# First-stage loads, squares and copies reordered, and the meta keys' V products paired in 64-row halves, in a Hymba encoder block on 8 cores

## The reference

```python
h = rms_norm(x, norm_g)
u, g_pool, q, k, v, g_na = split(h @ w_in)                 # 1024 columns each
pool_out = pool_mixer(u, w_pool, pool_scale) * silu(g_pool)
# per query: softmax over 16 meta keys and a window of 8 rows x 16 columns of a grid 64 wide
p = softmax(concat([s_meta, s_grid]))                       # 16 heads of 64
na_out = (p_m @ vm + p_g @ v_window) * silu(g_na)
y = rms_norm(x + concat([pool_out, na_out]) @ w_out, final_g)
```

## Time and profile before

| what | value |
|---|---|
| median of 3 runs | 1763.38 us (1757.53 to 1893.18) |
| the profiled execution | 1761.12 us |
| its span, slowest core (core 0) | 1759.6 us |
| spans of the 8 cores | 1748.7 to 1759.6 us |
| mean granted TensorE clock of core 0 | 0.986 of full speed |
| busy: PE, DVE, ACT, POOL | 96%, 57%, 47%, 7% |
| attention stage, as the windows cut it | 442 to 1059 us |

### The profile page before, as it was taken

One profiled execution on the slowest core, in us unless ns is written; L12 is line 12 of the kernel. 1 busy time (PEld: TensorE's weight loads), 2 busy tenths in 40 slices (PEclk: granted clock), 3 DMA queues, 4 the chain that ended last, 5 costly groups with the idle time before them and its releaser, 6 DMA issues.

```text
span 1759.6 us, 39346 instructions; the slowest of 8 cores (1748.7 to 1759.6 us)
## 1 busy us (share of the span) xinstructions
PE 1690.0 (96%) x13906; PEld 873.7 (50%) x13906; DVE 1000.9 (57%) x1907; ACT 821.3 (47%) x1219; POOL 124.3 (7%) x202
## 2 busy tenths in 40 slices
PE   7799999999999899999999998999999999999998
PEld 3344544444455555655666554444444444444443
DVE  3354544442466665766777755556655566556654
ACT  3256666331256765777777762332333233323332
POOL 1011021111100000000000020000000000000000
PEclk9899999999999999999999999999999999999999
DMA  9689778663555566666543479733454346524521
GB/s 264 218 239 282 226 240 238 200 169 136 172 141 157 149 166 176 154 179 176 146 123 98 132 214 266 187 114 109 126 174 148 86 128 162 168 88 129 139 96 61
DMA packets 163814, 289.21 MB, mean 164 GB/s; under 512 B 70627, under 2 KB 92643, under 8 KB 155047
## 3 DMA queue, kind: packets, MB, share of 16 engines
q1 hardware_dynamic: 110167, 155.04, 31.2%
q0 software_dynamic: 37184, 95.66, 19.1%
q10 hardware_dynamic: 16272, 35.99, 6.6%
HBM read 194.90 MB, written 100.90 MB: 168 GB/s over the span
## 4 chain that ended last, share of the span: by engine, by line
PE 79%; issue 5%; ACT 5%; DVE 4%; DMA 4%; SPq 2%; ACTq 1%; DVEq 0%; POOL 0%; POOLq 0%
PE bankpair L433 19%; PE bankpair L927 9%; PE bankpair L588 9%; PE bankpair L620 9%; PE bankpair L407 9%; PE bankpair L380 9%; PE bankpair L904 5%; PE bankpair L1039 3%; PE bankpair L1008 3%; ACT sb_PT L1014 2%; DMA sb_XSG<-xt 2%; DVE sb_PT L1020 1%; PE bankpair L567 1%; PE bankpair L368 1%; DVE sb_QT L217 1%
## 5 line engine op out<-in xcount | busy, mean ns | idle before, releaser
L1014 ACT ACTIVATE sb_PT<-bankpair 128x1024 bf16<-128x1024 f32 (+1 forms) x368 | 318.8, 921 | 152.8 <-PE bankpair L1008 112.1
L433 PE MATMUL bankpair<-sb_Wo,sb_MIX 128*128 128x512 bf16 x1536 | 336.9, 381 | 3.7 <-DVE sb_MIX L417 3.7
L433 PEld LDWEIGHTS bankpair<-sb_Wo,sb_MIX 128*128 128x128 bf16 x1536 | 150.8, 98 | 187.8 <-issue 9.1
L1020 DVE TENSOR_TENSOR sb_PT<-sb_PT,sb_FT 128x1024 bf16<-128x1024 bf16 (+1 forms) x264 | 174.8, 666 | 106.1 <-ACT sb_PT L1014 103.3
L927 PE MATMUL bankpair<-sb_Wz,sb_HT 128*128 128x512 bf16 x768 | 199.6, 388 | 3.0 <-ACT sb_PM L957 2.7
L588 PE MATMUL bankpair<-sb_HT,sb_Wk 128*128 128x512 bf16 (+1 forms) x832 | 189.7, 383 | 9.5 <-ACT sb_Wk L219 5.0
L904 PE MATMUL bankpair<-sb_HT,sb_Wq 128*128 128x512 bf16 x768 | 194.7, 382 | 1.7 <-DVE sb_QT L217 1.7
L620 PE MATMUL bankpair<-sb_Wv,sb_HT 128*128 128x512 bf16 x816 | 184.0, 379 | 0.0
L380 PE MATMUL bankpair<-sb_HT,sb_Wg 128*128 128x512 bf16 x768 | 182.6, 381 | 0.0
L441 ACT ACTIVATE sb_junk<-sb_Y 128x1024 bf16<-128x1024 f32 x48 | 50.7, 1057 | 266.3 <-DVE sb_Y L436 266.3
L407 PE MATMUL bankpair<-sb_HT,sb_Wg 128*128 128x512 bf16 x768 | 167.7, 379 | 0.0
(11 more groups left out here) (104 smaller groups left out, 1736.3 us busy)
## 6 DMA issues: line engine op xcount, KB each, us to landing
sb_X<-xall SPq DMA_DIRECT2D x51, 512.0 KB, 5.7
sb_XR<-xall SPq DMA_DIRECT2D x48, 512.0 KB, 3.6
y<-sb_O POOLq DMA_DIRECT2D x48, 512.0 KB, 3.2
sb_HT<-hT_s SPq DMA_DIRECT2D x23, 1024.0 KB, 6.1
sb_KR<-kT_s SPq DMA_DIRECT2D x14, 1024.0 KB, 7.2
sb_UW<-u_s SPq DMA_DIRECT2D x54, 256.0 KB, 7.8
kT_s<-sb_KTs POOLq DMA_DIRECT2D x13, 1024.0 KB, 5.1
v_s<-sb_Vs POOLq DMA_DIRECT2D x49, 260.0 KB, 3.5
```

What stands on the lines that cost most here:

```text
L433: S.op('tensor', lambda e, po=po, kc=kc, cg=cg, j=j: e.matmul(banks[po][:, :], MIX[:, kc, j * 128:(j + 1) * 128], Wo[kc // 4][:, kc % 4, c ...
L1014: S.op('scalar', lambda e: e.activation(out=PT[ps][0:nk, bi, :, 0:n].rearrange('p (a b) q -> p a b q', a=2), in_=bank2[sp][0:nk, :].rearra ...
L1020: S.op('vector', lambda e: e.tensor_tensor(out=PT[ps][0:nk, bi, :, 0:n], in0=PT[ps][0:nk, bi, :, 0:n], in1=bl['E'](hs), op=ALU.mult), read ...
```

## The change

**Start of stage 1.** The constants' DMAs leave the start and go into the loop at its index 3 (the scaling of `psc` to index 7); `hT` of chunk 0 is written after the transposes of chunk 1 begin; the K products of chunk 0 and the transposes of chunk 1 are interleaved; the first V column group of chunk 0 is computed as soon as its two weights are there, then the first half of K of chunk 1, and then the second V column group. The fillers between chunk 1's transposes are gone. The SP queue has the same loads in the same order.

**Loop of stage 1.** `p1_front` is split: `p1_sum` (load, square, root) runs two row tiles ahead, `p1_scale` one ahead. `p1_HTevac` is issued directly behind the transposes, and no longer behind the K products and tables.

**Attention.** The heads' banks are now cut by halves (heads 0 to 3 and 4 to 7 of a G) in place of parity. The meta product of a unit becomes two matmuls of 64 rows and 260 columns, one in each half of the array, into banks 4 and 5, issued beside the K products. `pv_plan` takes the place of `pv_steps` and says, by the number of blocks of the next unit and by whether that unit begins a pair, where the meta products go, which product opens a bank, and in which step each half is done. The V products of the corner cells use 128 rows always, with the missing half of `VC` set to zero. The output's store goes on SP's queue for all tiles.

```diff
@@ -552,12 +550,19 @@
...
+
+        def p1_scale(ci, j):
+            xs, sc = tile_xs[(ci, j)], tile_sc[(ci, j)]
...
+
+        def p1_front(ci, j):
+            p1_sum(ci, j)
+            p1_scale(ci, j)
...
@@ -693,30 +698,42 @@
...
-        p1_consts()
+        p1_wcast(0)
+        p1_wcast(1)
+        p1_K(0, [0, 1])
+        p1_wcast(2)
+        p1_front(1, 0)
+        p1_K(0, [2, 3])
+        p1_wcast(3)
+        p1_front(1, 1)
+        p1_K(0, [4, 5])
+        p1_T(1, 0)
+        p1_K(0, [6])
+        p1_HTevac(1, 0)
+        p1_front(1, 2)
+        p1_T(1, 1)
+        p1_K(0, [7])
+        p1_HTevac(1, 1)
+        p1_front(1, 3)
+        p1_wcast(4)
+        p1_T(1, 2)
+        p1_HTevac(1, 2)
         p1_keep(0)
-        p1_wcast(0)
+        p1_sum(2, 0)
+        p1_wcast(5)
+        p1_VU(0, 0, (0,))
+        p1_T(1, 3)
+        p1_scale(2, 0)
+        p1_HTevac(1, 3)
+        for j in range(1, 4):
+            p1_VU(0, j, (0,))
+        p1_sum(2, 1)
+        p1_K(1, [0, 1])
+        p1_wcast(6)
+        p1_wcast(7)
+        p1_K(1, [2, 3])
         for j in range(4):
...
+            p1_VU(0, j, (1,))
...
@@ -725,22 +742,27 @@
             ntc = chunks[ci][1]
             nxt = order[idx + 1] if idx + 1 < len(order) else None
             ntn = chunks[nxt][1] if nxt is not None else 0
-            if idx > 1:
-                p1_keep(ci)
+            p1_keep(ci)
+            if idx == 3:
+                p1_consts()
+            if idx == 7:
+                S.op('vector', lambda e: e.tensor_scalar(out=psc[:], in0=psc[:], scalar1=0.5, scalar2=None, op0=ALU.mult),
+                     reads=['psc'], writes=['psc'])
             for j in range(4):
                 if j < ntn:
                     p1_T(nxt, j)
                     if (nxt, j) in after:
-                        p1_front(*after[(nxt, j)])
-                if idx > 1:
+                        p1_scale(*after[(nxt, j)])
+                        if after[(nxt, j)] in after:
+                            p1_sum(*after[after[(nxt, j)]])
+                    p1_HTevac(nxt, j)
+                if idx > 1 or j > 1:
                     p1_K(ci, [2 * j, 2 * j + 1])
                 if idx >= 2 and j % 2 == 1 and tpi < len(pieces):
                     p1_table(tpi); p1_table(tpi + 1)
                     tpi += 2
                     if tpi < len(pieces):
                         p1_tload(tpi); p1_tload(tpi + 1)
-                if j < ntn:
-                    p1_HTevac(nxt, j)
                 if j < ntc:
                     p1_VU(ci, j)
                 if idx in (4, 5):
@@ -1021,59 +1046,65 @@
                 out=PT[ps][0:nk, bi, :, 0:n], in0=PT[ps][0:nk, bi, :, 0:n], in1=bl['E'](hs), op=ALU.mult),
                  reads=[('PT', ps, bi), bl['eres']], writes=[('PT', ps, bi)])
-        def p2_pvmeta(ui, par):
+        def p2_pvmeta(ui, opens, ends=False):
             t, s, G = units[ui]
...
+            for half in range(2):
+                rows = slice(64 * half, 64 * half + 64)
+                S.op('tensor', lambda e, half=half, rows=rows: e.matmul(
+                    banks[4 + half][:, 0:260], PM[t % 2][rows, G, s, :], VMb[rows, G, 0:260],
+                    start=(opens or half == 1), stop=(ends and half == 0)), reads=[('PM', t % 2, G)] + VMR, writes=[PS(4 + half)])
+
+        def p2_pv(ui, half, bi, opens, last):
             t, s, G = units[ui]
-            n = TILES[t]['nq'] * 16
             ps = ui % 2
             bl = unit_blocks(units[ui])[bi]
-            nk = bl['nk']
-            for jj in range(4):
+            for q in range(4):
+                jj, par = 2 * half + q // 2, q % 2
                 h = 2 * (4 * G + jj) + par
...
+                S.op('tensor', lambda e, q=q, jj=jj, par=par, h=h: e.matmul(
+                    banks[4 + half][:, q * 65:(q + 1) * 65], PT[ps][:, bi, par * 4 + jj, :],
+                    bl['V'][:, h * 65:(h + 1) * 65], start=(opens and q == 0), stop=(last and q == 3)),
+                     reads=bl['vres'] + [('PT', ps, bi)], writes=[PS(4 + half)])
+
+        def p2_norm(ui, half):
             t, s, G = units[ui]
             tl = TILES[t]
             n = tl['nq'] * 16
             at = (ui // 2) % 2
-            ab = 4 + par
+            ab = 4 + half
             accv = lambda: banks[ab][0:n, 0:260].rearrange('p (a b) -> p a b', a=4)
-            rs = slice(par * 4, par * 4 + 4)
+            rs = slice(half * 4, half * 4 + 4)
+            c0 = (8 * G + 4 * half) * 64
             S.op('vector', lambda e: e.reciprocal(rec[0:n, rs], accv()[:, :, 64]),
-                 reads=[PS(ab)], writes=[('rec', par)])
+                 reads=[PS(ab)], writes=[('rec', half)])
             S.op('vector', lambda e: e.tensor_tensor(
-                out=ATT[at][0:n, :].rearrange('p (a b c) -> p a b c', a=8, b=2)[:, 4 * G:4 * G + 4, par, :], in0=accv()[:, :, 0:64],
+                out=ATT[at][0:n, c0:c0 + 256].rearrange('p (a c) -> p a c', a=4), in0=accv()[:, :, 0:64],
                 in1=rec[0:n, rs].unsqueeze(2).to_broadcast([n, 4, 64]), op=ALU.mult),
-                 reads=[PS(ab), ('rec', par)], writes=[('ATT', at)])
-            if G == 1 and par == 1:
+                 reads=[PS(ab), ('rec', half)], writes=[('ATT', at)])
+            if G == 1 and half == 1:
                 t0 = tl['t0']
-                late.append(lambda: S.op('gpsimd' if 9 <= t < 13 else 'sync', lambda e: e.dma_start(
+                late.append(lambda: S.op('sync', lambda e: e.dma_start(
                     out=at_d[t0:t0 + n * 4, :].rearrange('(r c) f -> r c f', c=64)[:, 16 * s:16 * s + 16, :], in_=ATT[at][0:n, :]),
                      reads=[('ATT', at)], writes=[('at_d', t, s)], dma=('sA', at)))
...
+        nblk = [len(unit_blocks(u)) for u in units]
+        first_step = [sum(nblk[:i]) for i in range(len(units))]
+
+        def pv_plan(ui):
+
+            nb = nblk[ui]
+            nn = nblk[ui + 1] if ui + 1 < len(units) else 2
+            even = ui + 1 == len(units) or first_step[ui + 1] % 2 == 0
+            opens = even and nn == 2
+            lead = [lambda bi=bi: p2_pv(ui, 0, bi, bi == 0 and not opens, False) for bi in range(nb - 1)]
+            tail = lambda last: [lambda: p2_pv(ui, 0, nb - 1, False, last)]
+            half1 = [lambda bi=bi: p2_pv(ui, 1, bi, False, bi == nb - 1) for bi in range(nb)]
+            n0, n1 = [lambda: p2_norm(ui, 0)], [lambda: p2_norm(ui, 1)]
+            if nn == 2:
+                return 0 if even else 1, opens, {0: lead, 1: tail(True) + n0 + half1 + n1}
+            if even:
+                return 2, False, {0: lead, 1: tail(False), 2: half1 + n1}
+            return 1, False, {0: lead, 1: tail(True) + n0 + half1[:2], 2: half1[2:] + n1}
         late = []
         for fc in range(KC):
@@ -1107,11 +1138,8 @@
             if b == 1:
                 while late:
                     late.pop(0)()
-            for f in pv_steps(ui - 1)[b] if ui > 0 and b < 3 else []:
+            for f in pv_plan(ui - 1)[2].get(b, []) if ui > 0 else []:
                 f()
...
             if b == nb - 1:
                 unit_end(ui)
@@ -1147,10 +1175,18 @@
             for ui, b in steps[k:k + 2]:
                 if b == 0:
                     unit_begin(ui)
+                if b == 2 and ui > 0 and pv_plan(ui - 1)[0] == 2:
+                    p2_pvmeta(ui - 1, False, True)
+                    p2_norm(ui - 1, 0)
+            for ui, b in steps[k:k + 2]:
                 p2_qk(ui, b)
             for ui, b in steps[k:k + 2]:
+                if b < 2 and ui > 0 and pv_plan(ui - 1)[0] == b:
+                    p2_pvmeta(ui - 1, pv_plan(ui - 1)[1])
+            for ui, b in steps[k:k + 2]:
                 unit_step(ui, b)
-        for part in pv_steps(len(units) - 1):
+        p2_pvmeta(len(units) - 1, True)
+        for part in pv_plan(len(units) - 1)[2].values():
             for f in part:
                 f()
         while late:
```

More of the change, by code:

```diff
@@ L241, in build_program @@
         second += [('VP0_%d' % q, [128, VW], BF16) for q in range(3)] + [('VC%d' % w, [128, VW], BF16) for w in range(2)]
-        second += [('VMb', [128, 2, 2, 4, 65], BF16), ('KM', [128, KC, 32], BF16), ('HTm', [128, KC, 128], BF16)]
+        second += [('VMb', [128, 2, 264], BF16), ('KM', [128, KC, 32], BF16), ('HTm', [128, KC, 128], BF16)]
         second += [('PM%d' % i, [128, 2, 4, 128], BF16) for i in range(2)]
@@ L491, in p1_consts @@
                     S.op('gpsimd', lambda e: e.dma_start(out=psc[:], in_=psT_d), writes=['psc'], dma='c6')
-                    S.op('vector', lambda e: e.tensor_scalar(out=psc[:], in0=psc[:], scalar1=0.5, scalar2=None, op0=ALU.mult),
-                         reads=['psc'], writes=['psc'])
                     S.op('gpsimd', lambda e: e.dma_start(out=mbP[:], in_=mbP_d), writes=['mbP'], dma='c9')
@@ L541, in p1_load, with p1_sum @@
                          writes=[('X', xs)], dma=('X', xs))
[L543 removed]
+                def p1_sum(ci, j):
                     if (ci, j) not in tile_xs:
```

(11 more changed lines are left out.)

44 lines of the change are left out of this document (removed).

## The result

The changed kernel is slower: its time is 1.0325 times that of before, with a 95% interval of 1.0304 to 1.0347. Its profiled execution took 1821.2 us, 60.1 more than the profiled execution of before (1761.1); the forecast was 1803. Two of its four executions were disturbed and are left out of the ratio.

A forecast was written before the change was run, and what follows sets the result against it. The prediction took the PE, busy 96% of the span, as the bound; -3 - 9 - 12.3 - 1.5 (corner products and mode switches) + 12 + 41 + 15 = +42 on 1761.1 gave 1803 us, own range 1790 to 1818, 8-in-10 range 1765 to 1832.

The forecast's parts named there:

- one wait as the decisive one: Attention, two-chunk tiles: V products of the moved second half wait for DVE's multiply of the next unit's block 0; +41 us.
- Rival 2: Attention: the block-0 wait doesn't bind, so the kernel is not slower; 1747 us, chance 0.08.
- rival 3: Whole kernel: every wait costs the clock (+34 us) and DMA gives nothing back at the start; 1831 us, chance 0.15.
- rival 1: Start, loop and clock: x comes in time and the clock mostly holds; 1782 us, chance 0.27.
- Rival 4: Attention: the two meta halves don't run together, +12 us on the forecast; 1815 us, chance 0.05.
- Banks opened early: Attention, tiles 0 and 4, 15 places: meta pairs right behind K products wait 1.0 us for the division; +12 us.
- Start: Start of stage 1: loads land earlier without the constants, but the PE idles 8 us awaiting chunk 2's x; -3 us.
- The constants at index 3: Loop of stage 1: constants loaded there have a whole chunk, 29 us, before the first fold needs Wp; no cost.
- Waits of the transposes: Loop of stage 1: the four waits for the HT copy go, with their clock loss; -9 us, bounds -4 and -11.
- Meta pairs: Attention: two 64-row halves run at once, so 112 products of 0.11 us are saved; -12.3 us.
- Clock: Attention: half of the 20 long block-0 waits drop the PE's clock; +15 us, bounds 0 and +34.
- "Other edits": Attention: zeroing half of VC and the store on SP's queue cost nothing, at worst 4 and 2 us.

The follow-up runs named there:

- slot3: The changed kernel, with block 0 of a pair's second step written to the free fourth buffer slot at s = 0 (12 of 24 places); 1798.6 us, ratio 1.0226.
- early_pair: The changed kernel, with the meta pair opening both banks in the first step also before 3-block units, blocks 0 and 1 read in step 1; 1811.0 us.
- stage1_only: The kernel before with the stage 1 edits alone, attention as before; 1760 us, ratio 0.9997.
- s1_early: stage1_only with the constants' DMAs at index 2, ahead of the WuT loads, and the HT copy ahead of the scaling on DVE; 1752.6 us, ratio 0.9933.
- best1: s1_early with ACT's table pieces behind p1_VU and the memsets of KM, PM and VMb on POOL; 1747.4 us, ratio 0.9900.
- mid_full: Stage 1 of before, changed attention, but at 39 places two 128-row meta products, each before its half, blocks 0 and 1 read in step 1; ratio 1.0065.
- full_all: mid_full with no meta product paired: all 112 units use two products of 128 rows; ratio 1.0039.
- best_pair: best1 with the attention of mid_full and VC[0] of tile 0 zeroed on POOL; 1749.8 us, ratio 0.9922.

## Why the prediction was right, and which terms were off

**Right in kind and place.** The forecast named one wait as the decisive one, at 24 places, for +41 us. It is there 24 times, with 39.4 us, and slot3 takes half of it away with half of its cause. The single values hold as well: 1.65 us forecast at s = 0 of tile 9, 1.64 measured. The place costs a little more than its wait, though. From the start of the five fill products to that of the V products behind them it is 1.09 us before (852.26 to 853.35) and 2.89 after (897.12 to 900.01), 1.80 more, where the forecast had 1.65 and 0.05 for the restart: the row counts the idle time only from the end of the last fill product. Rival 2 (1747 us, the wait doesn't bind) is refuted. Rival 4 (the halves don't run together) is too: the group of meta products, 224 in both, held the PE for 61.7 us and now does so for 36.0.

```profile
L1053 PE MATMUL bankpair<-sb_VMb,sb_PM 64*128 64x260 bf16 x224 | 36.0, 281 | 16.4 <-DVE sb_rec L1078 11.0 <-DVE sb_ATT L1080 5.0 <-issue 0.3
```

**The time was met less well than the mechanism.** 1818 us by the ratio and 1821 in the profiled execution lie at or past the upper end of the forecast's own range (1790 to 1818), and nearer to rival 3 (1831) than to 1803. But rival 3 isn't what happened: it had nothing gained at the start and 34 us of clock. Nor is rival 1 (1782): the loop's gain of 11 us didn't come. By stage, on the two slowest cores, the time stands against the forecast like this: the start 2 us better; the loop of stage 1 18 worse (-9 forecast, 15.8 - 6.9 = +8.9 measured); the second stage 6 worse (-12.3 - 1.5 + 12 + 41 + 15 = +54 forecast, +60 from its first Q product to the first product of the third stage, 621.3 to 681.6 us); the third stage 4 better (701.5 to 697.7), which no term had. So what the forecast missed is mostly the loop of stage 1, and not the attention.

**Banks opened early: +12, about right.** The waits of the meta products are 16.4 us in 30 entries, against 7.1 before, 9.3 more. By the lengths of the tiles 0 and 4 the change costs 4.7 and 12.4 us there, which holds the clock's share too. What I had not drawn from it is that the same price falls due wherever such a pair is put right behind K products; early_pair showed that.

**Start: -3, measured -5.1.** x of chunk 2 was there at 56.75 (57.1 forecast), and the K products of chunk 1 began at 60.69 (61.1). The PE had idled 3.6 us by then and not 8, since the first V group ran later than forecast, from 48.1 to 57.1 with the last transposes in it. The loop's first transposes came at 76.2, where 81.3 on like terms and 77.8 in the forecast stood.

```profile
56.75 1.06 ACT L547 ACTIVATE sb_junk<-sb_X 128x1024 bf16<-128x1024 f32 x1 [11.82 <-DMA sb_X<-xall]
...
58.66 0.75 DVE L559 TENSOR_SCALAR sb_XN<-sb_X,sb_rstd 128x1024 bf16<-128x1024 f32 x1
...
60.69 1.67 PE L593 MATMUL bankpair<-sb_HT,sb_Wk 128*128 128x512 bf16 x5 [3.61 <-DVE sb_HT L580]
```

**The constants at index 3: a cover that was not there.** The step "have a whole chunk (29 us) before the first fold needs `Wp`" failed. `Wp` was issued at 135.84 and landed 35.5 us later. On POOL's queue the last of four loads of `WuT`, the stores of a chunk's `kT` and `hT` (1 MB each), one of V and the eight small constants had not landed by then, and the core's 16 DMA engines were busy 90% or more in nearly every slice of 128 to 172 us. The PE stood for 6.6 us on this core (9.3 in stage1_only); with the issue ahead of the `WuT` loads the wait is gone (s1_early). The forecast had named what it would cost if the cover failed, and put no number to it.

```profile
sb_Wp<-w_pool POOLq DMA_DIRECT2D x1, 512.0 KB, 35.5
```

**Waits of the transposes: -9, measured -0.7.** They stood at 7.5 us in the loop and stand at 6.8, in three places. The copies have the places that I had counted on, but the waits have other reasons. For the longest, 3.07 us, it is this: a V copy on ACT stands behind a table piece that waits for its own DMA, and DVE's list waits for that copy. ACT, then DVE, then the PE:

```profile
277.28 1.28 ACT L672 ACT_TABLE_LOAD   x1 [6.09 <-DMA sb_STG<-xt]
...
282.46 0.59 ACT L219 CAST sb_Vs<-bankpair 128x512 bf16<-128x512 f32 x1 [0.51 <-ACT sb_XT L672]
```

```profile
283.15 0.69 DVE L217 CAST sb_Vs<-bankpair 128x512 bf16<-128x512 f32 x1 [10.11 <-ACT sb_Vs L219]
...
284.69 1.22 DVE L580 TENSOR_TENSOR sb_HT<-bankpair,sb_gTs 128x1024 bf16<-128x1024 f32 x1
```

```profile
286.05 0.61 PE L572 MATMUL bankpair<-sb_ident,sb_XN 128*128 128x128 bf16 x8 [3.07 <-DVE sb_HT L580]
```

Even the bound of -4 was too good. best1 moves the table pieces, and the wait of this place, 4.0 us in s1_early, is gone. The other two (1.69 and 2.09 us, beside the narrower products of chunk 12) stay there with 1.78 and 2.09, so the table pieces aren't their reason; it stays open. The clock adds to it: in the loop it lost 8.5 us (the time at a lower clock times the missing share), and 3.4 before.

**Meta pairs: -12.3.** By the 0.10 us a pair of the timelines it is 112 x 0.10 = 11.2 us. The runs don't show that as a gain: with 73 of the pairs mid_full isn't faster than full_all, and in the second stage the PE's busy time didn't fall (592.6 us from 436.9 to 1059 before, 599.8 in the last window above), though the lower clock lengthens it and may hide a gain. The -1.5 for the corner products was not measured by itself.

**Clock: +15, measured +14 on the slowest core, partly by luck.** What a lower clock costs is the span times what is missing in its mean: 1819.7 x 0.021 = 38 us against 1759.6 x 0.014 = 25. These are the two slowest cores; in the mean of the eight it is 29 against 22. The term stood for the waits of the second stage, and there the clock lost 9.7 us more on these two cores, 9 in the mean; the rest is the loop's 5 and smaller shifts. The reason was too simple as well. I had half of the long waits cost the clock. Over the eight cores of the trace there are 198 waits of V products on the multiply, with 29 falls of the clock behind them (within 2 us of the wait's end), one in seven: none behind the 54 of 1.6 to 1.8 us (s = 0), 13 behind the 72 near 1.85 (s = 3), and 14 behind the 24 of 2.0 to 2.1 (tiles 3 and 12, with fewer fill products). So within this kind more falls stand behind the longer waits, but 59 of the 72 near 1.85 us left the clock alone. It fell also behind 13 of 54 idle times of 1.0 to 1.3 us of any kind in the second stage. The Trainium skill, TensorE: Matmul & The Clock Gate, section A second HAM failure mode: psum-queue depth-cycling, says that frequent short idles between groups let the clock swing; the 13 falls behind idles under 1.3 us agree with it. What decides between two idles of one length no run here shows.

**"Other edits": nothing, or 4 and 2 us at worst.** Both covers failed. The memset costs 1.2 us of wait and 1.3 us of clock at one place, since the first Q copy stands behind it in DVE's list, however idle DVE is on average. The store costs 4 to 6 us in tile 12 where POOL's queue lets the next weights go early. The sum for the slowest core: the forecast's 42, less 2 for the start, plus 8 for the transposes, 7 for `Wp`, 1 for the meta pairs, 1 for the Q copy (its clock is in the clock's term), some 3 in tile 12, less 3 for the block-0 waits and the clock, is 57 of the 60 measured. What the other 3 are stays open; the restarts of the block-0 places (24 times 0.1 us) would be 2 of them. The 3 in tile 12 are the mean growth of 6.4 less the two block-0 waits of that tile.

## What to carry to other kernels

Where two steps share a pair, ask for each read that is moved back by a step whether the next step's first write has been emitted ahead of it: the price is the whole chain of the new block, and half of the moved reads gives half of it back. A product that opens an accumulation bank belongs behind work that needs no bank, not right behind the last user's division. And an instruction or transfer that costs nothing by the average load must be priced at its place: what stands behind it in that engine's list or queue, and which later transfers of the queue it leaves were held back by it.

## What the hardware showed that I had not expected

- A store moved from POOL's queue to SP's let POOL issue the next stage's weights 45 us earlier (982.6 in full_all for 1027.7 before), and four loads on SP's queue then took 13.5 us to issue (15.4 in best_pair) in place of 5.8. The Trainium skill, Trainium Kernel Development and Optimization, section Key Constraints, says that the queues share the same DMA engines and that several of them only save issue time. That SP's loads took longer while POOL's were under way agrees with the sharing; the rows add that a queue is also an order, which the kernel before leaned on without saying so.
- A load of 512 KB on POOL's queue took 35.5 us to land where a load of the same size, two stores of 1 MB, one of 260 KB and eight small loads ahead of it had not landed yet; the loads of x on SP's queue, of the same size, took 10.4 us in that stretch (128 to 172 us) and 7.3 in the median of all 51. Issued 36 us earlier, ahead of the same loads (s1_early), it took 17.7.
- A pair of 64-row products of 260 columns takes 0.12 us beside other 64-row products and 0.31 by itself, and one of 128 rows takes 0.11.
